# Order of VectorE's work in a bidirectional scan, input states in four transfers, and the last expert block's rows added by a 0/1 product

## The reference, cut to what matters

```python
h = layer_norm(x, ln_in_g, ln_in_b)              # first work on the input, 512 x 1024
...
xs, log_a, bm, cm = ssd_direction_inputs(xbc, dt_raw, dt_bias, a_log, d)   # per direction d
lmat = exp(segsum(a)); cb = cm @ bm^T            # within a chunk of 128 tokens
y_diag = (cb * lmat) @ xs
states = bm^T @ (decay_states * xs)              # carried from chunk to chunk
y_off = (cm @ prev_states) * exp(a_cs)
y = y_fwd + y_bwd + d_skip * x_heads
...
y_slots = run_block(...) * slot_gate             # one block of up to 128 tokens per expert
out = zeros.at[slot_tok].add(y_slots)            # every token gets its 4 experts' rows
x = x + g2 * out
return rmsnorm(x, final_norm_w)
```

## Time and profile before

| | us |
|---|---|
| median of 3 runs | 3627.0 (3624.52 to 3628.54) |
| profiled execution | 3625.36 |
| its span in the trace | 3623.6 |
| PE busy | 3418.1 (94%) |
| DVE busy | 2428.2 (67%) |
| ACT busy | 1685.2 (47%) |

### The profile page before, as it was taken

How to read it: one execution, slowest core, us unless ns; L and a number is a source line. 1 busy time by engine, 2 the same in 40 slices (tenths; PEclk the granted TensorE clock), 3 DMA queues, 4 the chain that set the end, 5 groups by cost and what they waited for, 6 DMA issues and landing times.

```text
span 3623.6 us, 43697 instructions
## 1 busy us (share of the span) xinstructions
PE 3418.1 (94%) x13658; PEld 2377.7 (66%) x13658; DVE 2428.2 (67%) x2964; ACT 1685.2 (47%) x2233; POOL 476.0 (13%) x626
## 2 busy tenths in 40 slices
PE   7989999999989999998998899989999999999996
PEld 3444588874344588874654554378888888888884
DVE  3565564553665554455556884179999999999995
ACT  2333332232333332233221123168888888888884
POOL 0000000000000000000000000033343433334340
PEclk9988999999988999999998999999999999999998
DMA  4100233332110333332111003279999999999995
GB/s 182 53 25 34 87 116 114 114 105 70 47 37 22 94 116 117 111 111 75 47 58 53 24 24 95 65 259 368 358 379 359 368 364 369 370 364 376 352 373 179
DMA packets 167696, 618.85 MB, mean 171 GB/s; under 512 B 18496, under 2 KB 18624, under 8 KB 166880
## 3 DMA queue, kind: packets, MB, share of 16 engines
q1 hardware_dynamic: 156768, 573.84, 44.3%
q0 software_dynamic: 10816, 43.52, 4.2%
HBM read 587.92 MB, written 29.36 MB: 170 GB/s over the span
## 4 chain that ended last, share of the span: by engine, by line
PE 53%; issue 21%; POOL 11%; DVE 9%; ACT 3%; POOLq 2%; DMA 1%; DVEq 0%; SPq 0%; ACTq 0%
PE bank L586 52%; POOL pick L552 2%; POOL sb_work L498 2%; POOL y_rows L558 1%; DVE sb_rstd L1727 1%; DVE sb_work L1769 1%; POOL sb_work L504 1%; POOL picks_e L505 1%; POOLq L511 1%; POOL sb_work L544 1%; POOL sb_work L546 1%; POOLq L510 1%; POOL sb_work L541 1%; DVE sb_turn_tables L2262 1%; DVE sb_work L2266 1%
## 5 line engine op out<-in xcount | busy, mean ns | idle before, releaser
L2469 DVE TENSOR_TENSOR w_part<-sb_ring,w_part 128x1024 fp32r<-128x1024 f32 x762 | 888.5, 1225 | 58.2 <-ACT w_part L1631 43.1
L1631 ACT ACTIVATE w_part<-sb_ring 128x1024 fp32r<-128x1024 f32 x762 | 769.1, 1053 | 74.8 <-PE bank L1123 50.9
L1123 PE MATMUL bank<-w_part,xg_hi 128*128 128x512 f32 x2048 | 564.0, 397 | 0.0
L586 PE MATMUL bank<-h_hi,split_part 128*128 128x512 f32 x1408 | 444.9, 400 | 4.7 <-ACT h_hi L1399 4.7
L1123 PEld LDWEIGHTS bank<-w_part,xg_hi 128*128 128x128 f32 x2048 | 383.1, 188 | 89.3
L586 PE MATMUL bank<-sb_work,sb_ring 128*128 128x512 f32 (+5 forms) x880 | 331.6, 531 | 4.0 <-ACT sb_probe L1197 2.6
L1123 PE MATMUL bank<-w_part,xg_lo 128*128 128x512 f32 x1024 | 321.3, 395 | 0.0
L586 PEld LDWEIGHTS bank<-h_hi,split_part 128*128 128x128 f32 x1408 | 265.3, 190 | 68.4 <-ACT h_hi L1399 5.1
L1123 PE MATMUL bank<-w_part,act_hi 128*128 128x512 f32 x1024 | 284.8, 400 | 1.1 <-DVE act_lo L2512 0.6
L586 PE MATMUL bank<-sb_hT,sb_ring 128*128 128x512 f32 (+1 forms) x608 | 273.6, 608 | 8.2 <-ACT sb_hT L1216 8.2
L586 PE MATMUL bank<-h_lo,split_part 128*128 128x512 f32 x704 | 272.2, 394 | 0.0
(11 more groups left out here) (350 smaller groups left out, 4593.9 us busy)
## 6 DMA issues: line engine op xcount, KB each, us to landing
sb_ring<-in_w SPq DMA_DIRECT2D x768, 512.0 KB, 7.5
sb_ring<-in_wstream SPq DMA_DIRECT2D x304, 512.0 KB, 3.6
y_rows<-sb_padc POOLq DMA_DIRECT2D x1, 4096.0 KB, 27.4
sb_xT<-in_x SPq DMA_DIRECT2D x1, 2048.0 KB, 11.3
x_rows<-sb_padc SPq DMA_DIRECT2D x1, 2048.0 KB, 22.6
residual<-sb_hT POOLq DMA_DIRECT2D x1, 2048.0 KB, 6.6
sb_hT<-residual POOLq DMA_DIRECT2D x1, 2048.0 KB, 7.9
x_rows<-sb_work SPq DMA_DIRECT2D x1, 2048.0 KB, 6.6
```

Source lines behind the costliest of these rows:

```text
L586: ins = nc.tensor.matmul(out, l, r, start=start, stop=stop)
L1123: ins = nc.tensor.matmul(out[n][:], l[:, k, :], r[:, n * 512:(n + 1) * 512], start=False, stop=(k, p) == (KD - 1, 2))
L1631: nc.scalar.activation(w_hi[t % SPLITS], ring[:, t % RING, :], ACT.Copy).then_inc(s_hi, 1)
L2469: nc.vector.tensor_tensor(w_lo[t % SPLITS], ring[:, t % RING, :], w_hi[t % SPLITS].bitcast(F32), ALU.subtract).then_inc(s_lo, 1)
```

## The change

Opening: `x` comes in four transfers, each with its own semaphore, ahead of the small parameters; PE waits per transfer, and for the constants alone before that. Positions and rows have a semaphore of their own, waited for by DVE after the first norm. The fill of `x_rows` stands behind ring tile 9 on SP's queue; the fill of `y_rows` waits for the third projection (`cq1`).

Scan: DVE's order in an `x` step is new, with four buffers for scaled carries in place of two (two of them in the tile `rstd`). No instruction is added or dropped.

End: the last block's rows are not added in memory. SP loads `y_rows` when the blocks before the last have been added. DVE makes `last_rows`, which is 1 where a token is the one of the slot and 0 elsewhere, and PE adds `y_slot` times `last_rows` in the same bank in which it turns `y_rows` by plain products with the identity. The sums of squares are interleaved.

```diff
-            sp.dma_start(consts[:], io["consts"]).then_inc(s_in, 16)
+            sp.dma_start(consts[:], io["consts"]).then_inc(s_const, 16)
+            for i in range(4):
+                sp.dma_start(xT[:, 2 * i:2 * i + 2, :],
+                             io["x"].rearrange("p (k t) -> p k t", t=T)[:, 2 * i:2 * i + 2, :]).then_inc(s_x[i], 16)
             sp.dma_start(cols[:], io["cols"]).then_inc(s_in, 16)
-            sp.dma_start(xT[:], io["x"].rearrange("p (k t) -> p k t", t=T)).then_inc(s_in, 16)
...
+                if n == RING + 1:
+                    sp.wait_ge(dve_done, when("zeros"))
...
-            sp.wait_ge(s_put, last * 16 + 32)
+            sp.wait_ge(s_put, last * 16 + 16)
...
-            pool.wait_ge(dve_done, when("zeros"))
+            pool.wait_ge(pe_done, when("full", "proj", 0, "cq1"))
...
+                    for k in range(n):
+                        pe.wait_ge(s_x[k // 2], 16)
+                        mm(out[:], ones, src[:, k, :], k == 0, k == n - 1, *(("mean", tag) if k == n - 1 else ()))
...
+            pe.wait_ge(dve_done, when("last_rows"))
             for m in range(KD):
                 out = bank("sums", m)
+                if m % 4 == 0:
+                    pe.wait_ge(moe_act_done, in_turn(last, "y_kept", m // 4, more=False))
+                mm(out[:], y_slot[:, m * P:(m + 1) * P], last_rows, True, False)
+                if m == 0:
+                    pe.wait_ge(s_sum, 16 * TB)
                 for b in range(TB):
-                    ins = nc.tensor.transpose(out[:, b * P:(b + 1) * P], h2[:, b, m * P:(m + 1) * P], ident)
-                ins.then_inc(pe_done, did.up(("full", "sums", m)))
-            norm(("final",), None, 0, KD, ones_d, center=False)
+                    mm(out[:, b * P:(b + 1) * P], h2[:, b, m * P:(m + 1) * P], ident, False, b == TB - 1,
+                       *(("sums", m) if b == TB - 1 else ()))
+                if m >= 2:
+                    running("var", ("final",), sq, m - 2, ("square", ("final",)))
...
                     seg_arg(0)
                     seg_arg(1)
+                    dve.wait_ge(pe_done, when("full", "cb", s))
...
+                    nc.vector.tensor_tensor(by_head(xs), by_head(xsrc), per_head(dt, blk, d),
+                        ALU.mult).then_inc(dve_done, did.up(("xs", s)))
                     decayed(0)
+                    seg_arg(2)
+                    scaled_carry(0)
+                    scaled_carry(1)
+                    decayed(1)
+                    seg_arg(3)
+                    scaled_carry(2)
+                    scaled_carry(3)
+                    decayed(2)
+                    add_within(0)
+                    decayed(3)
+                    dve.wait_ge(dve_done, did.n)
+                    nc.vector.tensor_tensor(by_head(xw), by_head(xsrc), per_head(wdec, blk, d),
+                        ALU.mult).then_inc(dve_done, did.up(("xw", s)))
+                    add_within(1)
                     for g in range(GROUPS):
...
+                        add_carried(g)
+                    for g in (2, 3):
+                        add_within(g)
...
+            nc.vector.tensor_scalar(last_rows, iota, row_next, None, ALU.is_equal).then_inc(dve_done,
+                did.up(("last_rows",)))
```

More of the change, by code:

```diff
@@ L161, in build @@
         s_ctx = sem("context_loaded")
+        s_x = [sem(f"x_part{i}_loaded") for i in range(4)]
+        s_pos = sem("positions_and_rows_loaded")
+        s_const = sem("constants_loaded")
         s_res = sem("residual_moved")
@@ L282, in build @@
         wdec = dt_raw
-        yoffs = turn_tables[:, :, 0:GW]
+        yoffs = [a[:, i, 0:GW] for a in (turn_tables, rstd) for i in range(2)]
         rs_tok = sb("rs_tok", [P, TB])
@@ L342, in build @@
         idx_next, idx_cur = region(1).bitcast(I32), region(1).bitcast(I32)
+        last_rows = turn_tables[:, 0, :]
         slot_row = region(TB)
@@ L633, in norm @@
             def norm(tag, src, at, n, ones, center=True, width=T):
-                if center and tag[0] in ("in", "cfm"):
+                if center and tag[0] == "in":
+                    out = bank("mean", tag)
+                    for k in range(n):
+                        pe.wait_ge(s_x[k // 2], 16)
+                        mm(out[:], ones, src[:, k, :], k == 0, k == n - 1, *(("mean", tag) if k == n - 1 else ()))
+                if center and tag[0] == "cfm":
                     pe.wait_ge(dve_done, when("norm_in", tag))
@@ L2253, in add_within, with scaled_carry, add_carried @@
                             did.up(("free", "yd", s, g)))
+                    def scaled_carry(g):
+                        dve.wait_ge(pe_done, when("full", "yoff", s, g))
+                        dve.wait_ge(dve_done, did.n)
+                        nc.vector.tensor_tensor(by_head(yoffs[g]), by_head(bank_of("yoff", s, g)[:, 0:GW]),
+                            per_head(ecs, blk, d, HPG, g * HPG), ALU.mult).then_inc(dve_done, did.up(("free", "yoff",
+                            s, g)))
+                    def add_carried(g):
+                        yg = ytok[:, b, g * GW:(g + 1) * GW]
+                        dve.wait_ge(dve_done, did.n)
+                        nc.vector.tensor_tensor(yg, yg, yoffs[g], ALU.add).then_inc(dve_done, did.up())
```

76 lines of the change are left out of this document (30 added, 46 removed).

## The result

The changed kernel takes 3593.81 us (median of 4 runs, 3587.99 to 3601.02), the kernel before on the same chip 3625.76 (4 runs): a ratio of 0.9907, 95% interval 0.9893 to 0.9922. It is 32 us faster.

What follows compares the result with a forecast made beforehand. The prediction took TensorE, busy 94%, to bound the whole kernel, with VectorE setting the scan step. Opening 9.3, scan 12.5 and end 5.3 sum to 27.1 us: 3625.4 to 3598.3, given as 3600, range 3594 to 3608.

Steps and rivals of the forecast that it cites:

- opening: Program start: `x` in quarters without fills beside it starts the mean at 6.4, ends it at 15.1; gain 9.3 us.
- end: After the last block: no memory round trip, eight banks at 2.04 us, root at 3602.1; gain 5.3 us.
- So gaps of 1.1 in place of 2.62: 1.5 us a step: Steady scan step: VectorE's three real gaps shrink to two, before decays 1 and 3; seven steps give 10.5 us.
- The layout from the issue of `seg` 0: Scan: one new step's TensorE and VectorE times, counted from TensorE's issue of `seg` 0, giving a step of 25.7 us.
- The banks don't bind: Scan: PSUM banks hold nothing up; the tightest, for `seg` 3, is free 0.6 us before it is needed.
- 16 if all three gaps go: Scan, upper bound of the gain: 2.62 x 7 = 18 us, stopped at 16 by TensorE's bound of 24.5 a step.
- The end of the scan: Third row squares: VectorE sets them instead of TensorE, whose 2.0 us in hand is gained too; 12.5 us for the scan.
- rival A: Opening: each quarter of `x` pays its own 2 us; gain 4.6 instead of 9.3, time 3604.6; chance 0.10.
- I take 1.18: End: price in us of a bank's four narrow products, taken from `cb`, making a bank 2.04 us.
- rival C: End: new products run at half clock throughout, costing 13 us instead of giving 5.3; time 3618; chance 0.05.
- Rival B: Scan: decays 1 and 3 wait a microsecond more, so a step gains nothing; time 3612; chance 0.07.
- Rival D: Opening's late fills: each microsecond of landing after 87.7 is lost; landing at 125 gives 3637; chance 0.02.

Runs made afterwards that it cites:

- the filled kernels: The changed kernel with one or two more 0.86 us products in TensorE's gate projection each scan step: steps of 25.25 and 26.11 us, against 24.89.

## Why the prediction was right or wrong

**The sum.** 27.1 was forecast and 33.3 measured: opening 1.3 less, scan 6.3 more, end 2.1 more, and 0.9 lost in stages that nothing touches and that differ by as much between profiles. So the time came out below the range by the scan and the end, and the opening's shortfall hid a part of it.

**The step that failed: "So gaps of 1.1 in place of 2.62: 1.5 us a step".** No gap was left, and a steady step gained 2.30. From the first to the last of the eight `x` steps' state additions are 174.24 us, where they were 190.71: 16.5 less, where 10.5 was forecast. That is 6.0 of the 6.3; the other 0.3 came from the first step. The layout from the issue of `seg` 0 was nearly right on TensorE's side: the exponentials of groups 1 and 3 end 6.28 and 11.79 us behind that issue, where 6.2 and 12.0 were laid out.

```profile
2078.49 0.19 PEld L592 LDWEIGHTS bank<-sb_ring,sb_xT 128*128 128x128 f32 x1 [0.24 <-issue]
2078.92 0.19 PEld L592 LDWEIGHTS bank<-sb_work,sb_consts 128*128 128x128 f32 x1 [0.24 <-DVE sb_work L2249]
```
```profile
2084.11 1.09 ACT L1579 ACTIVATE sb_work<-bank 128x384 f32<-128x384 f32 x2 [2.73 <-PE bank L592]
...
2089.62 1.09 ACT L1579 ACTIVATE sb_work<-bank 128x384 f32<-128x384 f32 x2 [1.79 <-PE bank L592]
```

(2084.11 + 1.09 and 2089.62 + 1.09, less 2078.92.) Wrong was where VectorE stood. The layout put decay 0 at 2.55; it is at 2082.37, 3.45, because VectorE is still at `xs`. With VectorE 0.9 later against TensorE, both gaps are covered (decay 1 has 0.62 us to spare, decay 3 0.28). The layout gave a step of 25.7 us in which TensorE worked 24.5 and waited for nothing: such a step can't repeat itself. TensorE gains on VectorE each time, until it has to wait for it. Where it waits, the rows of the same step show:

```profile
2088.62 0.30 PEld L592 LDWEIGHTS bank<-sb_work,sb_consts 128*128 128x128 f32 x2 [0.18 <-DVE sb_rstd L2270]
...
2089.22 0.34 PEld L592 LDWEIGHTS bank<-sb_work,sb_consts 128*128 128x128 f32 x2 [0.30 <-DVE sb_rstd L2270]
```
```profile
2092.01 1.55 PE L592 MATMUL bank<-sb_work 128*128 128x64 f32 x12 [0.17 <-DVE sb_work L2257]
2093.80 2.85 PE L592 MATMUL bank<-sb_work 128*128 128x384 f32 x8 [0.24 <-DVE sb_work L2301]
```

It is not `seg` 0 that waits: its 0.24 at 2078.92 is the ordinary distance of weight loads in the gate projection, as the load before it has it, and in the kernel with two more products it is 0.24 as well, although both arguments are done there 2.6 us before. The two halves of `seg` 3 wait for the banks of the third and fourth carry (so "The banks don't bind" fails with VectorE that late), the last products within the chunk for decay 3, and the state products for `xw`. One step was laid out and not carried to the state in which it follows itself.

The upper bound, "16 if all three gaps go", named the case; it lies in the text as a bound and had deserved to be the forecast. Its sum has slips. TensorE's terms as they are written add up to 24.8 and not to 24.5 (and measured, TensorE can do a step in 24.4, by the filled kernels). VectorE's step has 28 instructions, not 29. And its 22.52 busy and 2.0 of small gaps leave out that a gap that closes leaves the 0.10 us of a met wait: 22.53 busy and 2.36 between them are the 24.89 that were measured.

**The end of the scan: right.** The third row squares are held by VectorE and no longer by TensorE, and 2.0 us of the scan's gain lie behind its steps, as forecast (18.8, less 16.5 of the steps and 0.3 of the first).

```profile
2176.15 1.48 ACT L1596 ACTIVATE sb_sq<-sb_work 128x1536 f32<-128x1536 f32 x1 [1.59 <-DVE sb_work L2333]
```

**Opening: mechanism right, mis-sized by 1.3.** The first product is at 6.86, not 6.4, and the mean takes 9.46 us, not 8.70: TensorE's first six records come 0.85 us apart and only then 0.43, where before there were four. That number does not follow from the start: over all profiles the mean takes 8.72 to 10.11 us from a start at 6.7 to 6.9, and 8.70 to 9.76 from a start at 15.4 to 16.5. The last part of `x` was never waited for. That quarters and late fills both count was forecast in one term and is borne out for each.

The Trainium skill ("DMA: Bandwidth & Descriptors") has its rule to batch to at least 1 MiB in section "Bandwidth". It gives the fixed cost of some 2.0 us under "Anatomy of one DMA — SWDGE (gpsimd) path", for transfers that GpSimd issues; those of `x` are issued by SyncE. Against the rule, four parts of 512 KB brought the first projection 3.7 us forward of one of 2 MB, and rival A's 4.6 us of gain is out by 3.4. What a queued part costs no run shows, since TensorE waited for none but the first. The 421 GB/s of the earlier trace rows were not ring tiles alone: by the earlier trace rows the fill of `y_rows` ran until 29.8 us. But the kernel with `x` in one transfer, in which no fill runs from 13 to 20 us, moved 418 GB/s there with ring tiles of 512 KB.

**End: mechanism right, mis-sized by 2.1.** A bank costs 1.75 us, not 2.04: "I take 1.18" for four narrow products was the wrong one of two rows; with the transposes' 0.79 the text's own sum gives 8.4; four took 0.88, which gives 7.7, and 7.4 was measured. The load of `y_rows` was never waited for, and rival C (half clock, 13 us lost) did not come: 1.00 throughout.

**Rival B** (the gaps move) is out in the change, but the kernel with the arguments first alone is one in which waits stayed and cost more than B's price, by a mechanism that the forecast named for the end alone: the clock. **Rival D** is out: the fill landed at about 70, 17 us short of costing anything.

## What to carry to other kernels

Lay out a new order of a loop until it follows itself: give each engine its own work per step, let the one with less run ahead until it waits, and only then read the gaps. If your layout has an engine that waits for nothing and has less work than the step is long, it can't repeat: that engine will run ahead. (Every engine's sum may lie below a true step: the kernel before took 27.19 us with 22.52 on VectorE and some 24.4 on TensorE, since each waited for the other.) When work moves to another engine, look at which instruction of the first it will run beside, and start it beside those that read PSUM; here that choice was worth 1.7 us a step, the difference between row squares 4.6 us later and 9.1 us sooner than the changed kernel's.

## What the runs showed of the hardware that was not expected

- GpSimd's 2.76 us product (all in SBUF) stopped a VectorE instruction with all operands in SBUF for 2.56 us, and cost nothing beside VectorE additions that read PSUM banks (2.53 us either way).
- TensorE's clock fell to its lower level (1.2 of 2.4 GHz) behind a wait of 2.56 us in every scan step of one kernel from the third on, and stayed at the upper one through the same wait in its second and through 2.50 us in the steady steps of the kernel before, where it fell once, behind 2.54 us in the first step. A long wait is not needed either: with two more products it fell once behind waits of 0.26 and 0.24 us, after 19 us with TensorE 98% busy (state products 4.52 us in place of 2.85, clock 0.63). Filling 1.95 us of the wait with discarded products kept it at 1.00 and made the kernel 25 us faster.
- At the program's start TensorE's first four to seven records (512 columns) come 0.85 us apart and the others 0.43, whether it begins at 7 or at 16 us; the mean's 16 take 8.70 to 10.11 us over the seventeen profiles, and 9.46 and 9.99 in two of the same kernel. The clock column reads 1.00 there.
- A product with 128 moving columns costs 0.22 us, a quarter of one with 512 (0.86), where many follow one another.
